# A hybrid decoder block: eight more expert tiles beside the retrieval, two tile buffers instead of four beside the spreading, 80 of the gathered rows moved forward

## The chip, the cores and the metric

One core of one Trainium2 chip runs the whole block in one launch. The metric is device time in microseconds (us); of the kernel before, 3 runs gave a median of 3127.78 us (3124.86 to 3131.33). The core has five engines with a queue each: TensorE (PE, with weight loads shown as PEld), VectorE (DVE), ScalarE (ACT), GpSimd (POOL) and SyncE (SP), which here only issues transfers. Engines wait for one another through semaphores. A queue is worked off in order: while an instruction waits, all behind it wait too.

## The reference

A block of 1024 tokens of width 1024 passes gated linear attention, differential softmax attention and one output projection, and then a retrieval of experts (PEER). The change lies wholly in the last part:

```python
q = (xt @ w_q).reshape(T, 8, 2, 128)                 # 8 heads, 2 sets of sub-keys
s = jnp.einsum('thpd,hpkd->thpk', q, sub_keys)       # 128 scores for each
s_top, i_top = lax.top_k(s, 16)
cand_s = s_top[:, :, 0, :, None] + s_top[:, :, 1, None, :]
best_s, best_pos = lax.top_k(cand_s.reshape(T, 8, 256), 16)
g = jax.nn.softmax(best_s, axis=-1)                  # idx: 16 experts of 16384 for each head
h = jnp.einsum('td,ted->te', xc, jnp.take(u, ic, axis=0))
a = jax.nn.gelu(h, approximate=False) * gc
out = jnp.einsum('te,ted->td', a, jnp.take(v, ic, axis=0))
```

## The kernel before, in words

Of the 8 tiles of 128 tokens, the last 6 (768 tokens) are computed densely: for all 16384 experts, in 128 expert tiles of 128, `gelu(u x)` is multiplied by a dense table of weights that is zero where an expert was not picked, and then by `v`. The first 2 token tiles gather their rows: 256 rows of `peer_u` (128 picks for each of 2 tiles) and 256 of `peer_v`, 512 KB in each gather of 128 experts. Matmuls run on pairs of fp16 parts (three matmuls for one product, lines 238 to 240).

A *u part* of an expert tile is: load `u_in` (512 KB); turn it by 8 transposes (`turn`); ACT splits off `u_hi` and copies `u_all`; POOL forms `u_lo` (`low`); 2 halves of 24 matmuls (`hidden`); gelu. A *v part* is 36 matmuls into `y` for each expert tile. The u part needs no picks, so it can run early, its gelu kept in HBM (`early_tiles`) and read back later. Three stages matter:

- `retrieve` (about 620 to 994 us): for each of 8 heads PE computes queries and scores, and DVE picks (top 16 of the scores twice, candidates, top 16 of them, then index arithmetic); POOL multiplies `match`, DVE sums it. Beside it run 16 early tiles, two per head (`EARLY_R` * 8), one in the first, three in the last. Steps 1 to 3 of pairs of heads are loops.
- `spread_weights` (about 994 to 1526 us): 12 blocks of 64 tokens, each in 16 steps of 4 tokens. In a step DVE builds `same`, `right`, `left`, PE multiplies them into `tab`, ACT copies `tab` to `stage`, and SP stores 2 MB after 8 steps. Beside each block run 4 early tiles (48 in all): the halves of tile b come at steps 4b and 4b+2 of the block, and at step 4b, ahead of the first half, PE turns tile b+1. `EarlyTiles` has 4 buffers here, so that the tile which is turned was loaded a block ahead. SP does, in this order, `keep` (store a gelu, which waits for it) and `load` of the tile four further on. At the end two u tiles (`F.u_in`) for the next stage are turned and the first is multiplied.
- `experts` (about 1526 us to the end): 64 *late* tiles with u and v part, then 64 early ones with the v part alone, and 512 row jobs on DVE (6 per late tile, 2 per early tile), for which POOL issues gathers into 5 row buffers.

`E.turn` waits for `u_loaded`; `E.load` waits for the turn that frees its buffer; `E.keep` waits for `gelu_done`. The lines that the prediction follows:

```python
def turn(self, pe, c, b):
    pe.wait_ge(self.u_loaded[b], c * 16 + 16)
    pe.wait_ge(self.u_all_done, BASE + c * self.ring + b)
def keep(self, queue, c, b):
    queue.wait_ge(self.gelu_done, BASE + 2 * (c * self.ring + b) + 2)
```

Of the kernel before, what the change touches and what calls it, by code (L numbers as in the profile page):

```python
# [1338 lines left out]
EARLY_S = 4  # L1339
BLOCK = 64  # L1340
# [3 lines left out]
N_EARLY = EARLY_R * PEER_H + EARLY_S * NBLOCK  # L1344
# [108 lines left out]
def retrieve(nc, io, T):  # L1453
# [3 lines left out]
    with ExitStack() as ctx:  # L1457
        S = Space(nc, ctx, "r")
        E = EarlyTiles(nc, io, T, S, EARLY_R, 0, EARLY_R * PEER_H)
# [52 lines left out]
        PAIRS = PEER_H // 2  # L1512

        @block.sync
        def _(sp):
            w_v = io.w_peer_q[0].rearrange("(k p) (h c) -> h p k c", p=P, c=QDIM)

            def load_w(h):
                sp.dma_start(w_in[:], w_v[h]).then_inc(w_loaded, 16)

            def step(hh, b, first=False, last=False):
                h = 2 * hh + b
                if not last:
                    sp.wait_ge(w_lo_done, h + 2)
                    load_w(h + 2)
                if not (first and b == 0):
                    E.load(sp, h, 1)
                if not (last and b):
                    E.load(sp, h + 1, 0)
# [6 lines left out]
            for b in range(2):  # L1536
                step(0, b, first=True)
            with sp.Fori(1, PAIRS - 1) as hh:
                for b in range(2):
                    step(hh, b)  # L1540
            for b in range(2):
                step(PAIRS - 1, b, last=True)
            E.all_kept(sp, EARLY_R * PEER_H)

        @block.tensor
        def _(pe):
# [17 lines left out]
            def scores(h, sets=(0, 1)):  # L1564
                for m in sets:
                    pe.wait_ge(q_out, 4 * h + 2 * m + 2)
                    for g in range(2):
                        for j in range(4):
                            t = 4 * g + j
                            last = pe.matmul(bank[2 * m + g][:, j, :], q_t[:, m, t * P:(t + 1) * P],  # L1570
                                             keys_t[:, bass.ds(2 * h + m, 1), :].rearrange("p a k -> p (a k)"),
                                             start=True, stop=True)
                        last.then_inc(scored, 1)

            def step(hh, b, first=False, last=False):
                h = 2 * hh + b
                before = not (first and b == 0)
                if before:
                    E.turn(pe, h - 1, 1)
                else:  # L1580
                    E.turn(pe, h, 0)
                if not (last and b):
                    queries(h + 1, 1 - b)
                    scores(h + 1)
                if before:
                    E.hidden(pe, h - 1, 1, 0)
                    E.turn(pe, h, 0)
                    E.hidden(pe, h - 1, 1, 1)
                E.hidden(pe, h, 0, 0)
                if last and b:  # L1590
                    E.turn(pe, h, 1)
                E.hidden(pe, h, 0, 1)
                if last and b:
                    E.hidden(pe, h, 1, 0)
                    E.hidden(pe, h, 1, 1)
# [8 lines left out]
            for b in range(2):  # L1604
                step(0, b, first=True)
            with pe.Fori(1, PAIRS - 1) as hh:
                for b in range(2):
                    step(hh, b)
            for b in range(2):
                step(PAIRS - 1, b, last=True)  # L1610
            pe.wait_ge(index_done, BASE + 2 * PEER_H)
# [11 lines left out]
        def _(act):  # L1623
# [25 lines left out]
            def step(hh, b, first=False, last=False):  # L1649
                h = 2 * hh + b  # L1650
                before = not (first and b == 0)
                if before:
                    E.split(act, h - 1, 1)
                else:
                    E.split(act, h, 0)
                if not last:
                    split_w(h + 2, b)
                if not (last and b):
                    act.wait_ge(scored, 4 * h + 4)
                    queries_out(h + 1)  # L1660
                    scores_out(h + 1)
                if before:
                    E.gelu(act, h - 1, 1, 0)
                    E.split(act, h, 0)
                    E.gelu(act, h - 1, 1, 1)
                    E.keep(act, h - 1, 1)
                if last and b:
                    E.gelu(act, h, 0, 0)
                    E.split(act, h, 1)
                    E.gelu(act, h, 0, 1)  # L1670
                    E.keep(act, h, 0)
                    for half in range(2):
                        E.gelu(act, h, 1, half)
                    E.keep(act, h, 1)
                act.wait_ge(shifted, h + 1)
                nc.scalar.activation(weight[:], weight[:], ACT.Exp).then_inc(weighted, 1)
                if not (last and b):
                    for half in range(2):
                        E.gelu(act, h, 0, half)
                    E.keep(act, h, 0)  # L1680

# [9 lines left out]
            for b in range(2):  # L1691
                step(0, b, first=True)
            with act.Fori(1, PAIRS - 1) as hh:
                for b in range(2):
                    step(hh, b)
            for b in range(2):
                step(PAIRS - 1, b, last=True)
# [7 lines left out]
        def _(pool):  # L1705
# [6 lines left out]
            def step(hh, b, first=False, last=False):  # L1712
# [781 lines left out]
```

## Time and profile before

| | |
|---|---|
| median of 3 runs | 3127.78 us |
| profiled execution | 3127.37 us, its span 3125.7 us, so 1.67 us around it |
| PE busy | 2975.7 us (95%) |
| DVE busy | 2313.1 us (74%) |
| POOL, ACT busy | 1271.3 us (41%), 993.3 us (32%) |
| granted clock, mean | 0.976 |

Busy shares are means over stages with different limits, so the stretches in the section of rows below are to be read first, and then, within each stage, which engine never waits. The profile names tiles by stage: `r_` is the retrieval, `e_` the spreading, `f_` the experts, `x_` and `p_` are tiles that outlive a stage. In a row of a timeline stand the start, the length, the engine and line, and in brackets how long the engine had been idle before and what released it.

### The profile page before, as it was taken

Reading aid. Unit: us, or ns where it says so; the run is one execution under the profiler, and the core shown is the slowest. Engines: PE = TensorE matmul, PEld = TensorE weight load, DVE = VectorE, ACT = ScalarE, POOL = GpSimd, SP = SyncE. Lnnn points to the kernel's source line nnn. Section 1 sums busy time; section 2 is a strip of 40 time slices with the busy share of each in tenths; the row PEclk is TensorE's granted clock in tenths of the full one; section 3 lists DMA queues with packets and bytes.
Section 4 is the critical chain, followed back from the end, with each engine's and each line's share of the span. In section 5 each row is a group of like instructions: output and inputs, shape, how many; then the busy total and the mean of one; then the engine's idle time right before and its main releaser. Section 6 shows DMA issues by size and latency. Waiting matters only on the chain.

```text
span 3125.7 us, 48327 instructions
## 1 busy us (share of the span) xinstructions
PE 2975.7 (95%) x17450; PEld 1671.2 (53%) x17450; DVE 2313.1 (74%) x4671; ACT 993.3 (32%) x1420; POOL 1271.3 (41%) x875
## 2 busy tenths in 40 slices
PE   7989998899995999999679999999999999999999
PEld 4445464455553777777445555555555554444444
DVE  3355475369997666666388888888888888999996
ACT  4322364234432555555222222222222222222221
POOL 1013011034333121222266666666655655555562
PEclk9999899999997999999889999999999999999999
DMA  3110101212211455555598888888888878888884
GB/s 99 55 54 14 55 1 34 68 60 75 75 36 68 163 201 190 178 186 195 202 319 275 282 272 273 291 285 274 274 273 284 292 258 285 299 305 297 307 290 170
DMA packets 256176, 594.95 MB, mean 190 GB/s; under 512 B 20768, under 2 KB 127408, under 8 KB 252976
## 3 DMA queue, kind: packets, MB, share of 16 engines
q1 hardware_dynamic: 180016, 318.63, 30.3%
q0 software_dynamic: 73728, 268.47, 24.3%
q10 hardware_dynamic: 2304, 6.29, 0.6%
q8 instruction: 62, 1.02, 0.1%
q14 instruction: 66, 0.54, 0.1%
HBM read 513.63 MB, written 79.69 MB: 190 GB/s over the span
## 4 chain that ended last, share of the span: by engine, by line
PE 43%; DMA 3%; DVE 2%; issue 1%; SPq 1%; ACT 0%; POOL 0%; DVEq 0%; ACTq 0%
PE f_y L238 9%; PE f_y L240 9%; PE f_y L239 9%; PE f_hid L238 5%; PE f_hid L239 5%; PE f_hid L240 5%; DMA f_v_in<-in_peer_v 2%; PE f_u_ps L2181 2%; SPq L2147 1%; DMA f_g_in<-dense_weights 1%; DMA f_rows<-in_peer_u,p_row_index 1%; DVE f_rows L2320 1%; DVE p_h L2330 1%; DVE p_h L2312 0%; DVE f_a_lo L2362 0%
## 5 line engine op out<-in xcount | busy, mean ns | idle before, releaser
L238 PE MATMUL f_y<-f_v_hi,f_a_hi 128*128 128x512 f16 x1536 | 583.1, 380 | 12.8 <-DVE p_h L2312 12.7
L239 PE MATMUL f_y<-f_v_lo,f_a_hi 128*128 128x512 f16 x1536 | 582.9, 379 | 0.0
L240 PE MATMUL f_y<-f_v_hi,f_a_lo 128*128 128x512 f16 x1536 | 582.7, 379 | 0.0
L2279 POOL DMA_INDIRECT f_rows<-in_peer_u,p_row_index x256 | 354.2, 1383 | 210.2 <-DVE f_rows L2320 128.5
L2279 POOL DMA_INDIRECT f_rows<-in_peer_v,p_row_index x256 | 310.6, 1213 | 286.0 <-DVE p_h L2330 256.8
L2320 DVE SCALAR_TENSOR_TENSOR f_rows<-f_rows,p_xs 128x1024 f32<-128x1024 f32 x256 | 380.2, 1519 | 50.2 <-DMA f_rows<-in_peer_u,p_row_index 50.2
L2330 DVE SCALAR_TENSOR_TENSOR p_h<-f_rows,f_row_a,p_h 128x1024 f32<-128x1024 f32 x256 | 397.9, 1554 | 20.8 <-DMA f_rows<-in_peer_v,p_row_index 13.9
L2312 DVE SCALAR_TENSOR_TENSOR p_h<-f_y,p_h 128x512 f32<-128x512 f32 x384 | 263.2, 685 | 105.6 <-PE f_y L240 103.3
L2290 POOL TENSOR_TENSOR f_v_lo<-f_v_in,f_v_hi 128x1024 f16<-128x1024 f32 x128 | 281.3, 2197 | 143.9 <-ACT f_v_hi L2254 142.6
L238 PE MATMUL f_hid<-p_act_hi,x_u_hi 128*128 128x384 f16 x1008 | 330.4, 328 | 2.0 <-DVEq L2297 2.0
L239 PE MATMUL f_hid<-p_act_lo,x_u_hi 128*128 128x384 f16 x1008 | 330.4, 328 | 0.0
L240 PE MATMUL f_hid<-p_act_hi,x_u_lo 128*128 128x384 f16 x1008 | 330.0, 327 | 0.0
L1929 DVE TENSOR_TENSOR e_right<-p_iota,p_picked_all 128x512 f16<-128x512 f32 x192 | 138.6, 722 | 181.4 <-PE e_tab L1951 181.4
L1417 POOL TENSOR_TENSOR e_u_lo<-e_u_all,e_u_hi 128x1024 f16<-128x1024 f32 x48 | 106.7, 2223 | 403.7 <-ACT e_u_all L1411 403.7
L238 PEld LDWEIGHTS f_y<-f_v_hi,f_a_hi 128*128 128x128 f16 x1536 | 150.4, 98 | 198.0 <-DVE p_h L2312 21.8
L238 PE MATMUL e_hid<-p_act_hi,e_u_hi 128*128 128x384 f16 x768 | 251.3, 327 | 4.5 <-POOL e_u_lo L1417 4.5
L239 PE MATMUL e_hid<-p_act_lo,e_u_hi 128*128 128x384 f16 x768 | 251.4, 327 | 0.0
L240 PE MATMUL e_hid<-p_act_hi,e_u_lo 128*128 128x384 f16 x768 | 251.3, 327 | 0.0
L240 PEld LDWEIGHTS f_y<-f_v_hi,f_a_lo 128*128 128x128 f16 x1536 | 150.5, 98 | 181.6 <-issue 0.8
L239 PEld LDWEIGHTS f_y<-f_v_lo,f_a_hi 128*128 128x128 f16 x1536 | 150.5, 98 | 176.1 <-issue 0.7
L2261 ACT ACTIVATE f_a_hi<-x_gel 128x768 f16<-128x768 f32 x128 | 107.7, 841 | 332.6 <-DVE x_gel L2354 258.9
L2254 ACT ACTIVATE f_v_hi<-f_v_in 128x1024 f16<-128x1024 f32 x128 | 134.8, 1053 | 196.7 <-DMA f_v_in<-in_peer_v 191.6
(314 smaller groups left out, 5343.0 us busy)
## 6 DMA issues: line engine op xcount, KB each, us to landing
f_v_in<-in_peer_v SPq DMA_DIRECT2D x128, 512.0 KB
dense_weights<-e_stage SPq DMA_DIRECT2D x24, 2048.0 KB, 8.6
f_g_in<-dense_weights SPq DMA_DIRECT2D x32, 1536.0 KB
x_u_in<-in_peer_u SPq DMA_DIRECT2D x64, 512.0 KB
e_u_in<-in_peer_u SPq DMA_DIRECT2D x48, 512.0 KB
x_gel<-early_tiles SPq DMA_DIRECT2D x64, 384.0 KB
early_tiles<-e_gel SPq DMA_DIRECT2D x48, 384.0 KB, 2.5
a_w_in<-in_w_in SPq DMA_DIRECT2D x24, 512.0 KB, 3.7
```

The costliest lines, as they stand in the source:

```text
L238: pe.matmul(out, a_hi, b_hi, start=first, stop=False)
L239: pe.matmul(out, a_hi, b_lo, start=False, stop=False)
L240: return pe.matmul(out, a_lo, b_hi, start=False, stop=last)
L1417: self.nc.gpsimd.tensor_tensor(self.u_lo[b][:], self.u_all[:], self.u_hi[b][:], ALU.subtract).then_inc(self.u_lo_done, 1)
L1929: nc.vector.tensor_tensor(right[r][:], lanes(T.iota[:], 1, P, BANK_T, P), lanes(key1_t[:, toks], 2, P, BANK_T, P), ALU.is_equal)
L2254: nc.scalar.activation(v_hi[g][j][:], v_in[m % 2][:], ACT.Copy).then_inc(v_hi_done, 1)
L2261: nc.scalar.activation(a_hi[g][j][:], gel[m % 2][:], ACT.Copy).then_inc(a_hi_done, 1)
L2279: nc.gpsimd.indirect_dma_start(out=rows[q % ROWS][:], out_offset=None, in_=table, in_offset=bass.IndirectOffsetOnAxis(ap=T.row_index[:, ti ...
L2290: nc.gpsimd.tensor_tensor(v_lo[g][j][:], v_in[m % 2][:], v_hi[g][j][:], ALU.subtract).then_inc(v_lo_done, 1)
L2312: nc.vector.scalar_tensor_tensor(T.h[:, NS + t, cols], y[k % 2][:], 1.0 / S_A, T.h[:, NS + t, cols], ALU.mult, ALU.add).then_inc(y_added, 1)
L2320: nc.vector.scalar_tensor_tensor(row, row, 1.0, T.xs[:, tile, :], ALU.mult, ALU.mult, accum_out=row_hid[:, tile, pick:pick + 1]).then_inc( ...
L2330: nc.vector.scalar_tensor_tensor(T.h[:, tile, :], row, row_a[:, tile, pick:pick + 1], T.h[:, tile, :], ALU.mult, ALU.add).then_inc(row_use ...
```

## The change

- `retrieve` has 24 early tiles in place of 16, given to the heads as 2, 3, 2, 3, 3, 2, 3, 6 (`HEAD_TILES`), and is written out by heads instead of looped. POOL's picks of head h now come in step h+1, behind the first tile's `low`, and the totals of the weights after the next head's first top 16.
- `spread_weights` has 2 buffers of early tiles in place of 4 (`EARLY_RING`), still 4 tiles per block; `right` is built from fp16 copies; DVE does 80 row jobs of the first token tile between its steps, POOL issues their gathers behind each `low`; two more u tiles are loaded for the next stage.
- `experts` has 56 late tiles and 72 early ones; its row jobs are 432, of which 288 lie in the late tiles (5.14 per tile instead of 6) and 2 in each early one. It starts with five rows and tiles 2 and 3 of u loaded, and its first load is `g_in`.

```diff
@@ -1337,11 +1337,17 @@
 EARLY_R = 2
 EARLY_S = 4
+EARLY_RING = 2
+ROWS = 5
+SPREAD_JOBS = 80
...
-N_EARLY = EARLY_R * PEER_H + EARLY_S * NBLOCK
+
+HEAD_TILES = (2, 3, 2, 3, 3, 2, 3, 6)
+N_RETRIEVE = sum(HEAD_TILES)
+N_EARLY = N_RETRIEVE + EARLY_S * NBLOCK
...
+            for h in range(PEER_H):
+                of_head = tiles(h)
+                E.turn(pe, *of_head[0])
+                if h + 1 < PEER_H:
+                    queries(h + 1, (h + 1) % 2)
+                    scores(h + 1)
+                for i, (c, b) in enumerate(of_head):
+                    E.hidden(pe, c, b, 0)
+                    if i + 1 < len(of_head):
+                        E.turn(pe, *of_head[i + 1])
+                    E.hidden(pe, c, b, 1)
...
+            for h in range(PEER_H):
+                of_head = tiles(h)
+                E.low(pool, *of_head[0])
+                if h + 2 < PEER_H:
+                    low_w(h + 2, h % 2)
+                if h:
+                    picks(h - 1)
+                for i, (c, b) in enumerate(of_head[1:]):
+                    E.low(pool, c, b)
+                    if h and i == 0:
+                        weights(h - 1)
+            picks(PEER_H - 1)
+            weights(PEER_H - 1)
...
-        E = EarlyTiles(nc, io, T, S, EARLY_S, EARLY_R * PEER_H, EARLY_S * NBLOCK)
+        E = EarlyTiles(nc, io, T, S, EARLY_RING, N_RETRIEVE, EARLY_S * NBLOCK)
+
+        def ring_at(blk, b):
+
+            return blk * (EARLY_S // EARLY_RING) + b // EARLY_RING, b % EARLY_RING
...
+                for q in range(SPREAD_JOBS * n // ALL, SPREAD_JOBS * (n + 1) // ALL):
+                    row_job(q)
...
                         if half == 0 and b + 1 < EARLY_S:
-                            E.turn(pe, blk, b + 1)
+                            E.turn(pe, *ring_at(blk, b + 1))
                         elif half == 0 and not last:
-                            E.turn(pe, blk + 1, 0)
-                        E.hidden(pe, blk, b, half)
+                            E.turn(pe, *ring_at(blk + 1, 0))
+                        E.hidden(pe, *ring_at(blk, b), half)
...
+            for n in range(BLOCKS_TILES):
+                E.low(pool, *ring_at(n // EARLY_S, n % EARLY_S))
+                upto = SPREAD_JOBS * (n + 1) // BLOCKS_TILES + ROWS if SPREAD_JOBS or n + 1 == BLOCKS_TILES else 0
+                for q in range(fetched, upto):
+                    fetch(q)
...
                 for b in range(EARLY_S):
-                    E.keep(sp, blk, b)
-                    if not last:
-                        E.load(sp, blk + 1, b)
+                    E.keep(sp, *ring_at(blk, b))
+                    if b + EARLY_RING < EARLY_S or not last:
+                        E.load(sp, *ring_at(blk, b + EARLY_RING))
...
-            for b in range(EARLY_S):
+            for b in range(EARLY_RING):
                 E.load(sp, 0, b, again=False)
...
+            for b in range(2):
+                rows = slice((N_EARLY + 2 + b) * P, (N_EARLY + 3 + b) * P)
+                sp.wait_ge(next_turned, b + 1)
+                sp.dma_start(F.u_in[b][:], io.peer_u[0, rows, :]).then_inc(next_loaded, 16)
...
+        LATE_JOBS = JOBS - SPREAD_JOBS - 2 * N_EARLY
...
-            return min(JOBS, 6 * late + 2 * early)
+            return min(JOBS, SPREAD_JOBS + LATE_JOBS * late // EARLY_FROM + 2 * early)
...
-                    if m % GROUP == 0 and not (first and m == 0):
+                    if m % GROUP == 0:
                         load_g(m // GROUP, n)
...
-                    elif not (first and m < 2):
+                    elif not (first and m < 4):
                         sp.wait_ge(u_turned, BASE + n - 1)
...
-            for q in range(ROWS):
-                fetch(q)
```

The change moves instructions on two queues that the prediction speaks of. On SP, at the start of the spreading, `e_u_in` is an early tile's load and `early_tiles<-e_gel` the store of a gelu. Before:

```order
L1387 DMA e_u_in<-in_peer_u 128x1024 x4
L2044 DMA x_u_in<-in_peer_u 128x1024 x2
L2045 UNCONDITIONAL_BRANCH
L2045 ISA
L1391 ISA
L1391 DMA early_tiles<-e_gel 128x768
L1386 REGISTER_ALU
L1387 ISA
L1387 DMA e_u_in<-in_peer_u 128x1024
```

With the change:

```order
L1393 DMA e_u_in<-in_peer_u 128x1024 x2
L2030 DMA x_u_in<-in_peer_u 128x1024 x2
L2031 UNCONDITIONAL_BRANCH
L2031 ISA
L1397 ISA
L1397 DMA early_tiles<-e_gel 128x768
L1392 REGISTER_ALU
L1393 ISA
L1393 DMA e_u_in<-in_peer_u 128x1024
```

The order of stores and loads is the same, but two tiles are loaded ahead of the first store and not four, so the load behind the store of tile n is that of tile n+2 and not n+4.

On POOL, in the last heads of the retrieval, `r_u_lo` is an early tile's `low`, `r_match` the picks and `r_picked` the weights of a head. Before:

```order
L1417 TENSOR_TENSOR r_u_lo<-r_u_all,r_u_hi 128x1024 x2
L1728 TENSOR_TENSOR r_match<-r_match,r_top_f 128x2048 x2
L1731 TENSOR_TENSOR r_picked<-r_weight,r_total 128x8x16
L1417 TENSOR_TENSOR r_u_lo<-r_u_all,r_u_hi 128x1024 x3
L1728 TENSOR_TENSOR r_match<-r_match,r_top_f 128x2048 x2
```

With the change:

```order
L1678 TENSOR_TENSOR r_match<-r_match,r_top_f 128x2048 x2
L1423 TENSOR_TENSOR r_u_lo<-r_u_all,r_u_hi 128x1024
L1683 TENSOR_TENSOR r_picked<-r_weight,r_total 128x8x16
L1423 TENSOR_TENSOR r_u_lo<-r_u_all,r_u_hi 128x1024 x4
L1678 TENSOR_TENSOR r_match<-r_match,r_top_f 128x2048 x2
```

The last head's picks now stand behind the `low` of all six of its early tiles, and the weights of the head before behind that of the second.

## Rows read from the trace of the kernel before

**Rows 1.** Windows: length; busy of PE, PEld, DVE, ACT, POOL; clock; DMA share, GB/s.
```profile
620.00:994.00 374.00, 344.26 (x1954) 200.32 (x1954) 332.23 (x1852) 137.45 (x175) 133.42 (x47) 0.96 0.18 60
994.00:1526.00 532.00, 518.85 (x4288) 364.09 (x4288) 329.09 (x775) 270.80 (x410) 106.69 (x48) 0.98 0.49 180
1526.00:1610.00 84.00, 47.10 (x248) 28.14 (x248) 54.07 (x70) 15.38 (x18) 51.50 (x37) 0.80 0.89 304
1610.00:2596.00 986.00, 985.77 (x5489) 544.48 (x5490) 827.24 (x953) 217.39 (x242) 610.61 (x421) 1.00 0.83 279
2596.00:3122.00 526.00, 519.17 (x2393) 232.60 (x2391) 472.35 (x451) 116.07 (x124) 283.95 (x183) 1.00 0.80 280
```

**Rows 2.** Timeline of one tile's end in the spreading, all engines.
```profile
1145.00 1.06 PE L1951 MATMUL e_tab<-e_right,e_left 128*128 128x128 f16 x16
1145.20 0.49 ACT L1436 ACTIVATE e_gel<-e_hid 128x384 f32<-128x384 f32 x1 [2.90 <-PE e_hid L240]
...
1145.88 0.33 SPq L1391 DMA_DIRECT2D early_tiles<-e_gel  x1
1145.90 1.04 PE L1401 MATMUL e_u_ps<-p_ident,e_u_in 128*128 128x128 f32 x8
...
1146.49 0.35 SPq L1387 DMA_DIRECT2D e_u_in<-in_peer_u  x1
```

**Rows 3.** Timeline of SP, the next tile.
```profile
1156.34 0.33 SPq L1391 DMA_DIRECT2D early_tiles<-e_gel  x1
1156.92 0.35 SPq L1387 DMA_DIRECT2D e_u_in<-in_peer_u  x1
1157.55 0.33 SPq L2037 DMA_DIRECT2D dense_weights<-e_stage  x1
```

**Rows 4.** Windows of 1 us behind the load of rows 2.
```profile
1149.00:1150.00 1.00, 1.00 (x8) 0.59 (x6) 0.06 (x1) 0.01 (x1) 0.91 (x1) 1.00 0.44 176
1150.00:1151.00 1.00, 1.00 (x12) 0.73 (x10) 0.00 (x0) 0.12 (x1) 1.00 (x1) 1.00 0.00 0
```

**Rows 5.** Timeline, a u load early in the experts stage.
```profile
1527.25 0.42 SPq L2150 DMA_DIRECT2D x_u_in<-in_peer_u  x1
...
1535.25 1.96 PE L2181 MATMUL f_u_ps<-p_ident,x_u_in 128*128 128x128 f32 x8 [4.31 <-DMA x_u_in<-in_peer_u]
```

**Rows 6.** Timeline, another idle time of PE.
```profile
1514.32 1.54 PE L1969 MATMUL e_u_ps<-p_ident,x_u_in 128*128 128x128 f32 x8 [2.37 <-DVE x_u_lo L1936]
```

**Rows 7.** Windows just behind the two idle times; PEclk is third from last.
```profile
1514.40:1518.00 3.60, 3.60 (x16) 2.32 (x17) 1.05 (x1) 1.02 (x1) 0.00 (x0) 0.56 0.86 364
...
1535.30:1538.70 3.40, 3.40 (x14) 2.47 (x15) 1.24 (x3) 0.00 (x0) 0.23 (x2) 0.50 1.04 400
```

**Rows 8.** Costliest groups of the page: gathers on POOL, row jobs on DVE.
```profile
L2279 POOL DMA_INDIRECT f_rows<-in_peer_u,p_row_index x256 | 354.2, 1383 | 210.2 <-DVE f_rows L2320 128.5
...
L2320 DVE SCALAR_TENSOR_TENSOR f_rows<-f_rows,p_xs 128x1024 f32<-128x1024 f32 x256 | 380.2, 1519 | 50.2 <-DMA f_rows<-in_peer_u,p_row_index 50.2
```

**Rows 9.** Chain of waits, late tiles: first and last of 58 turns.
```profile
1614.74 0.87 PE f_u_ps L2181 x8
...
2552.01 0.87 PE f_u_ps L2181 x8
```

**Rows 10.** Windows, one head of the retrieval.
```profile
821.90:864.30 42.40, 41.87 (x242) 24.20 (x241) 41.91 (x238) 17.09 (x21) 17.96 (x7) 1.00 0.20 69
```

**Rows 11.** Timeline of PE, the last head's scores.
```profile
917.12 3.73 PE L1570 MATMUL r_bank<-r_keys_t,r_q_t 128*128 128x128 f32 x32
```

**Rows 12.** Timeline of POOL at the end of the retrieval.
```profile
953.60 2.12 POOL L1417 TENSOR_TENSOR r_u_lo<-r_u_all,r_u_hi 128x1024 f16<-128x1024 f32 x1 [8.70 <-ACT r_u_all L1411]
962.84 2.12 POOL L1417 TENSOR_TENSOR r_u_lo<-r_u_all,r_u_hi 128x1024 f16<-128x1024 f32 x1 [7.12 <-ACT r_u_all L1411]
977.29 8.53 POOL L1728 TENSOR_TENSOR r_match<-r_match,r_top_f 128x2048 f16<-128x2048 f16 x2 [12.33 <-DVE r_match L1842]
```

**Rows 13.** Timeline of DVE, the last sum of the retrieval.
```profile
985.86 3.57 DVE L1788 TENSOR_REDUCE r_picked<-r_match 128x128 f32<-128x2048 f16 x1 [0.18 <-POOL r_match L1728]
```

More of the change, by code:

```diff
@@ L1511, in retrieve, with tiles @@
         block = ctx.enter_context(nc.Block())
-        PAIRS = PEER_H // 2
+        def tiles(h):
+            n = sum(HEAD_TILES[:h])
+            return [divmod(i, EARLY_R) for i in range(n, n + HEAD_TILES[h])]
         @block.sync
@@ L1535, in _ @@
             load_w(1)
[L1536 to L1543, printed above, removed]
+            for h in range(PEER_H):
+                if h + 2 < PEER_H:
+                    sp.wait_ge(w_lo_done, h + 2)
+                    load_w(h + 2)
+                for c, b in tiles(h):
+                    if c + 1 < N_RETRIEVE // EARLY_R:
+                        E.load(sp, c + 1, b)
+            E.all_kept(sp, N_RETRIEVE)
         @block.tensor
@@ L1570, in scores @@
                             last = pe.matmul(bank[2 * m + g][:, j, :], q_t[:, m, t * P:(t + 1) * P],
-                                             keys_t[:, bass.ds(2 * h + m, 1), :].rearrange("p a k -> p (a k)"),
-                                             start=True, stop=True)
+                                             keys_t[:, 2 * h + m, :], start=True, stop=True)
                         last.then_inc(scored, 1)
[L1575 to L1595, printed above, removed]
             for r in range(4):
@@ L1603, in _ @@
                 scores(0, sets=(m,))
[L1604 to L1611, printed above, removed]
+            for h in range(PEER_H):
[9 more added lines that the diff above has]
+                    E.hidden(pe, c, b, 1)
+            pe.wait_ge(index_done, 2 * PEER_H)
             pe.wait_ge(weight_done, PEER_H)
@@ L1647, in scores_out, with weigh @@
                                              ACT.Copy).then_inc(s_out, 1)
[L1649 to L1674, printed above, removed]
+            def weigh(h):
                 act.wait_ge(shifted, h + 1)
                 nc.scalar.activation(weight[:], weight[:], ACT.Exp).then_inc(weighted, 1)
[L1677 to L1680, printed above, removed]
             nc.scalar.activation(w_hi[0][:], w_in[:], ACT.Copy, scale=S_W).then_inc(w_hi_done, 1)
@@ L1690, in _ @@
                 scores_out(0, first=True, sets=(m,))
[L1691 to L1697, printed above, removed]
+            for h in range(PEER_H):
+                of_head = tiles(h)
+                E.split(act, *of_head[0])
+                if h + 2 < PEER_H:
+                    split_w(h + 2, h % 2)
+                if h + 1 < PEER_H:
+                    act.wait_ge(scored, 4 * h + 4)
+                    queries_out(h + 1)
+                    scores_out(h + 1)
+                for i, (c, b) in enumerate(of_head):
+                    E.gelu(act, c, b, 0)
+                    if i + 1 < len(of_head):
+                        E.split(act, *of_head[i + 1])
+                    E.gelu(act, c, b, 1)
+                    E.keep(act, c, b)
+                    if i == (len(of_head) - 2 if h + 1 == PEER_H else 1):
+                        weigh(h)
             for r in range(6):
@@ L1813, in step @@
                            for t in range(g * NT // 2, (g + 1) * NT // 2)] for g in range(2)])
-                if not (first and b == 0):
+                if h:
                     dve.wait_ge(weight_done, h)
@@ L1825, in step @@
                 c.step(nc.vector.tensor_scalar(row[0][:], part[:, 0, :], -1.0, 0.0, ALU.add, ALU.max))
-                if not (first and b == 0):
+                if h:
                     for n in range(2):
@@ L2058 @@
 NE = NKEYS
-ROWS = 5
 def experts(nc, io, T):
@@ L2367, in step @@
                 row_jobs(2)
+            lo_u(2, 2)
+            lo_u(3, 3)
             for n in range(NE):
@@ L2434, in allocate_first @@
     F.gel = [S.sb(f"gel{b}", [P, DSEQ], side="right") for b in range(2)]
+    F.rows = [S.sb(f"rows{b}", [P, D], side="right") for b in range(ROWS)]
     return F
```

206 lines of the change are left out of this document (106 added, 100 removed).

## The prediction

> **What bounds the kernel now.** I read the windows by stage first [rows 1]. In the retrieval PE is busy 344 of 374 us and DVE 332, so both are near their limit; in the spreading PE is busy 519 of 532 us and DVE only 329; in the experts stage PE is busy without a break in the late tiles (986 of 986) and nearly so in the early ones (519 of 526), while its first 84 us hold 47 us of work. So PE sets the end everywhere. A u part moved to another stage is worth something only where PE stood idle there, and any new idle time of PE costs its full length.
>
> Then I read one tile of the spreading on all engines [rows 2], because the change halves the buffers there. At 1145.00 PE ends the second half of tile n and multiplies two steps of tables; ACT does the gelu at 1145.20; SP stores it at 1145.88 and issues the next load at 1146.49; PE had begun the turn of tile n+2 at 1145.90. One tile later the store comes at 1156.34 [rows 3], a period of 10.46 us.
>
> **Spreading: the load now comes behind the turn that needs it.** Before, the load at 1146.49 was for tile n+4, with two more tile periods to land. With two buffers it is for tile n+2, and the code still turns tile n+2 at step 4(n+1), two steps behind the last half of tile n. That is the turn at 1145.90, 0.59 us ahead of the issue. SP cannot be earlier, since the load stands behind the `keep` of tile n, which waits for its gelu, which waits for PE. PE waits in order, and behind the turn stand the two halves of tile n+1 and its tables, so everything stops. It happens for tiles 2 to 47: 46 times.
>
> The wait per tile is 0.59 us plus issue to landing. Lower end: the store of 384 KB and the load of 512 KB move together until about 1149.4 (in 1149 to 1150 the transfers are at a share of 0.44, in the next us at 0.00) [rows 4], 2.9 us from issue, so 3.5 us. Upper end: a u load issued at 1527.25 behind two `v` loads, with gathers beside it, was waited for until 1535.25, 8.0 us [rows 5], so 8.6 us. In the changed spreading there are 1.67 gathers of 512 KB per tile beside the load, and every second load has the 2 MB store issued 0.63 us behind it [rows 3], but the mean share of the transfers was 0.49 [rows 1], not near 1 as in the rows of the upper end. I take 4.5 us, near the quiet end.
>
> The idle time costs clock as well. After PE had been idle 2.37 and 4.31 us [rows 5, 6], the granted clock was 0.56 and 0.50 in the next 3.6 and 3.4 us of full work [rows 7], that is the lower of its two levels (1.2 instead of 2.4 GHz) for nearly all of them: half of about 3.4 us, 1.7 us of work lost each time. I take 1.7 us per wait; the ends are 0 (the clock might stay up where waits come regularly) and 3.4 us (two such stretches).
>
> The Trainium skill, "TensorE: Matmul & The Clock Gate", section "HAM oscillation — how this bites in real kernels", describes a kernel in which a DMA wait per K-tile made every K-tile start at the lower clock, and prices it as the throttled time times one half. By that rule each of the 46 waits would pay; the two gaps of this trace agree, but no stretch here has gaps that repeat.
>
> The same notes, "DMA: Bandwidth & Descriptors", section "Anatomy of one DMA — SWDGE (gpsimd) path", give 2.0 us plus bytes / 436e3 (in us) for a transfer. For 512 KB that would be an estimate of 3.2 us, or 3.8 us of wait; this trace has 2.9 to 8.0 us, and the sum goes by these.
>
> Sum: 46 x (4.5 + 1.7) = 285 us. DVE does not replace PE as the bound: its 329 us plus 80 row jobs of 1.52 us [rows 8], 122 us, are 451 us in a stage of some 815 us. The two added u loads are issued with a u part of PE still ahead, 8.7 us (below), more than the 8.0 us of the upper end; cost 0, bound 5. The POOL gathers lie in idle time (107 of 532 us busy).
>
> **Experts: eight u parts fewer.** A late tile takes 16.44 us (58 turns from 1614.74 to 2552.01) [rows 9]. The early stretch of 526 us [rows 1] holds 64 tiles and the last group of 4, 68 v parts, 7.74 us each. So a u part is 8.70 us, and eight of them take 69.6 us off this stage: the 72 early tiles keep 2 row jobs each, as before, and the late ones have fewer, so PE stays the bound in both. The start is worth more than it looks: 84 us hold 47 us of PE work [rows 1], with the transfers at 0.89. Now five rows and two u tiles (3.5 MB) are there, `g_in` is loaded first, and 5.14 gathers per tile run instead of 6. At the stretch's 304 GB/s the 3.5 MB are 11.5 us, and 0.86 gathers of 0.52 MB less in five tiles another 7. I take 20 us; ends 0 and 37 (all idle time).
>
> **Retrieval: 8 u parts more.** In the middle heads PE is busy 41.87 of 42.4 us, with DVE at 41.91 [rows 10]. There a third tile lengthens the head by its full price, since PE had no room. Before the last head's scores (917.12) [rows 11] lay 11 tiles, now 15: at 8.7 to 9.24 us, 36 us later, 957 us for their end at 920.8. Behind them come 3 + 6 = 9 tiles. Tiles in a row take 9.24 us (`low` at 953.60 and 962.84) [rows 12], because `low` waits for the split and the next half for `low`: 83 us, so PE ends at 1040 us. DVE's index sums ended at 989.4 [rows 13], 68.6 us behind the scores; with the same distance they would end at 1026 (a few us later if DVE waits for the weights that now stand behind the `low` of the second tile), but its picks on POOL now stand behind the `low` of the sixth tile, at about 1032: 8.5 us of picks [rows 12] and one sum of 3.6 us [rows 13] make 1044.5. Against 989.4 that is 55 us. Ends: 40 (69.6 us of work less the 30 us for which PE was idle in the whole stage [rows 1]) and 62.
>
> So the move itself pays 70 + 20 - 55 = 35 us, and the halved buffers take 285.
>
> **Sum.** Against the profiled execution, 3127.4 us (its span and 1.7 us around it, 0.4 us under the median): 3127.4 + 285 - 69.6 - 20 + 55 = 3377.8 us, 8.0% slower.
>
> **Rivals.**
> 1. *Waits without the clock's share.* The clock stays high where matmuls return every 15 us. For it: in the middle of the retrieval, with short gaps, the clock is 1.00 [rows 10]. Against it: two of two gaps over 2 us [rows 7]. 46 x 4.5 = 207: 3300 us.
> 2. *Loads as slow as at the experts' start.* Gathers and the 2 MB store fill the transfers just when the u load is waited for: 46 x (8.6 + 1.7) = 474: 3567 us. Against it: the mean share of 0.49, and a longer period lowers it.
> 3. *POOL as a second wait.* Each `low` now stands behind gathers that wait for DVE's row jobs. If DVE lies less than a tile ahead, `low` comes late. `low` takes 2.12 us [rows 12] and the gathers 1.67 x 1.38 us [rows 8], 4.4 us per tile: at worst 46 x 4.4 = 202 more, 3580 us. Against it: during PE's wait DVE catches up, and POOL has over 10 us per tile.
> 4. *The other side: faster.* The wait for the load is hidden after all, because the load is issued or lands earlier than the turn. Then 3127.4 - 35 = 3093 us, 1.1% faster. It decides at 35 / 46 = 0.76 us of wait and clock per tile; over that the change loses. Against it stands that the issue alone is 0.59 us behind the turn [rows 2], and 3.5 us is the least a landing allows.
>
> **Chances.** Forecast (about 3378, from 3320 to 3450) 0.62; rival 1 0.18; rivals 2 and 3 together 0.16, much of it part of the way (3450 to 3530); rival 4 0.03; 0.01 for about no change. The range 3260 to 3500 takes in rival 1 with a gap of 3.7 us and leaves out the far parts of 2 and 3. Anything beyond 0.2% either way can be told from no change here: faster 0.03, same 0.01, slower 0.96.
>
> **What would show it.** In the waits of the changed profile, PE (or its weight loads) on line 1407, `e_u_ps`, waits for the load `e_u_in` 46 times, 4 to 5 us each; the period of the stores `early_tiles<-e_gel` is near 16.7 us, not 10.46; the clock of the spreading falls from 0.98 to near 0.85; the stage lasts some 815 us. The retrieval ends near 1050 us, with PE busy nearly to the end, and the last `r_match` behind the last `r_u_lo`. The experts stage has 52 steady periods of 16.44 us and starts its `f_y` within 65 us. If the store's period is still 10.5 us, the forecast is wrong at its root; if waits are there but the clock stays 1.00, it is rival 1.

## The result: 10.7% slower, and where the time went

The changed kernel takes 3465.47 us (median of 4 runs, 3451.03 to 3471.21) against 3126.86 us for the kernel before on the same chip: a ratio of 1.107, with a 95% interval of 1.104 to 1.111. The forecast was 3378 us with a range of 3260 to 3500. The profiled execution took 3451.03 us, so it is the shortest of the four; its span is 3449.3 us, 323.6 us over the span before (3125.7). The medians differ by 338.6 us: what the trace adds up to below is some 15 us less than the median.

First the page of the changed kernel: busy times, the granted clock by slices, the group of the turn and the landing of its load (last column of the last row, us from issue).

```profile
PE 3067.0 (89%) x17450; PEld 1719.2 (50%) x17450; DVE 2316.9 (67%) x4665; ACT 977.3 (28%) x1417; POOL 1266.7 (37%) x883
...
PE   7999889899996676667666699999999999999999
...
PEclk9999899999997888888888799999999999999999
...
L1407 PE MATMUL e_u_ps<-p_ident,e_u_in 128*128 128x128 f32 x384 | 91.9, 419 | 259.3 <-DMA e_u_in<-in_peer_u 258.2
...
e_u_in<-in_peer_u SPq DMA_DIRECT2D x48, 512.0 KB, 4.9
```

Eleven slices in the middle show a PE at six and seven tenths and a clock of 0.7 to 0.8: that is the spreading. The windows by stage (retrieval from 620, spreading, first part of the experts, late tiles, early tiles) answer to [rows 1]:

```profile
core 0: us, PE busy (x) PEld busy (x) DVE busy (x) ACT busy (x) POOL busy (x), PEclk, DMA share, GB/s
620.00:1050.00 430.00, 409.19 (x2385) 239.40 (x2382) 345.54 (x1851) 158.97 (x205) 145.63 (x55) 1.00 0.20 67
1050.00:1936.00 886.00, 621.36 (x4291) 420.56 (x4292) 421.70 (x937) 243.07 (x388) 183.85 (x133) 0.84 0.46 159
1936.00:2000.00 64.00, 37.32 (x222) 23.45 (x220) 42.18 (x57) 14.33 (x16) 39.18 (x25) 0.76 0.85 281
2000.00:2855.00 855.00, 855.00 (x4767) 472.40 (x4765) 670.33 (x739) 188.81 (x210) 488.07 (x324) 1.00 0.75 253
2855.00:3447.00 592.00, 584.65 (x2694) 261.79 (x2692) 536.67 (x510) 131.89 (x141) 324.84 (x208) 1.00 0.81 282
```

The spreading grew from 532 to 886 us. PE's busy time in it went from 519 to 621 us for nearly the same number of matmuls: each takes longer because the clock is 0.84, not 0.98. Its idle time went from 13 to 265 us. The waits of PE in that stretch name the cause (us in all, times, longest):

```profile
PE e_u_ps L1407 <- DMA e_u_in<-in_peer_u: 258.2, 47, 6.8
PE e_u_ps L1939 <- DVE x_u_lo L1906: 2.4, 1, 2.4
...
PE e_hid L238 <- POOL e_u_lo L1423: 1.1, 1, 1.1
```

The kernel before has this wait once, for the very first tile (4.8 us). One tile on SP, and the turn of PE that waits for its load, answer to [rows 2, 3]:

```profile
1365.03 0.33 SPq L1397 DMA_DIRECT2D early_tiles<-e_gel  x1
1365.64 0.35 SPq L1393 DMA_DIRECT2D e_u_in<-in_peer_u  x1
1382.12 0.33 SPq L1397 DMA_DIRECT2D early_tiles<-e_gel  x1
1382.70 0.35 SPq L1393 DMA_DIRECT2D e_u_in<-in_peer_u  x1
1383.34 0.33 SPq L2023 DMA_DIRECT2D dense_weights<-e_stage  x1
```

```profile
1381.26 1.06 PE L1921 MATMUL e_tab<-e_right,e_left 128*128 128x128 f16 x16
1389.06 1.97 PE L1407 MATMUL e_u_ps<-p_ident,e_u_in 128*128 128x128 f32 x8 [6.75 <-DMA e_u_in<-in_peer_u]
```

PE has nothing to do from 1382.3. The load is issued at 1382.70, with the 2 MB store 0.64 us behind it, and the turn starts at 1389.06, 6.36 us after the issue. The clock around this wait, before it, behind it and after:

```profile
1381.00:1389.00 8.00, 1.31 (x19) 1.04 (x17) 5.01 (x13) 1.53 (x3) 0.96 (x1) 0.87 0.76 236
1389.00:1393.40 4.40, 4.34 (x17) 2.93 (x18) 0.00 (x0) 1.94 (x2) 0.16 (x1) 0.50 0.88 376
1393.40:1398.00 4.60, 4.60 (x39) 3.10 (x38) 1.22 (x3) 1.53 (x3) 2.93 (x2) 0.97 0.17 24
```

For 4.4 us after the wait PE works at its lower level (0.50, that is 1.2 GHz), which costs 2.2 us. The turn itself takes 1.97 us there. It is so at every tile: in the trace's record of the granted clock the lower level follows each of the 47 waits, and PE works 2.7 to 6.1 us at it before the clock is back.

By the starts and ends of the same instructions in both traces, the 323.6 us are made of: up to the end of the retrieval +57.3 (`p_row_index` at 1046.80, was 989.5); spreading +351.5; from the last `e_tab` to the first `f_hid` -0.1; experts -85.0. The retrieval itself grew by more than 57.3: its first `r_bank` matmul starts at 619.4 here and at 624.8 before, so the stage is 62.7 us longer. The code ahead of it is the same in both, and in the traces of this study it ends anywhere from 616.8 to 625.3; a difference of a few us between the ends of one stage in two traces says little.

### The profile page after: what moved, and what is told of

The parts are those of the page before. It is cut to its first block and busy times, and to the rows that moved or that the text cites. A ratio compares the mean times of both kernels' runs of the same rounds, so it can differ in the third digit from the quotient of the medians.

```text
span 3449.3 us, 46781 instructions
## 1 busy us (share of the span) xinstructions
PE 3067.0 (89%) x17450; PEld 1719.2 (50%) x17450; DVE 2316.9 (67%) x4665; ACT 977.3 (28%) x1417; POOL 1266.7 (37%) x883
## 5 line engine op out<-in xcount | busy, mean ns | idle before, releaser
L1897 DVE TENSOR_TENSOR e_right<-e_iota,e_key 128x512 f16<-128x512 f16 x192 | 134.7, 702 | 435.3 <-PE e_tab L1921 435.3
L2287 POOL DMA_INDIRECT x_rows<-in_peer_v,p_row_index x256 | 316.1, 1235 | 273.2 <-DVE p_h L2337 245.7
L2337 DVE SCALAR_TENSOR_TENSOR p_h<-x_rows,f_row_a,p_h 128x1024 f32<-128x1024 f32 x256 | 394.0, 1539 | 9.8 <-DMA x_rows<-in_peer_v,p_row_index 2.8
L1407 PE MATMUL e_u_ps<-p_ident,e_u_in 128*128 128x128 f32 x384 | 91.9, 419 | 259.3 <-DMA e_u_in<-in_peer_u 258.2
L238 PE MATMUL f_hid<-p_act_hi,x_u_hi 128*128 128x384 f16 x880 | 287.8, 327 | 2.1 <-DVEq L2303 2.1
L240 PE MATMUL f_hid<-p_act_hi,x_u_lo 128*128 128x384 f16 x880 | 287.8, 327 | 0.0
L239 PE MATMUL f_hid<-p_act_lo,x_u_hi 128*128 128x384 f16 x880 | 287.7, 327 | 0.0
L2287 POOL DMA_INDIRECT x_rows<-in_peer_u,p_row_index x171 | 252.3, 1475 | 92.7 <-DVE x_rows L2327 53.1
L2327 DVE SCALAR_TENSOR_TENSOR x_rows<-x_rows,p_xs 128x1024 f32<-128x1024 f32 x176 | 268.0, 1560 | 9.0 <-DMA x_rows<-in_peer_u,p_row_index 8.9
L1407 PEld LDWEIGHTS e_u_ps<-p_ident,e_u_in 128*128 128x128 f32 x384 | 73.2, 218 | 266.8 <-issue 242.9
```

Of the source, the lines that this page charges most:

```text
L238: pe.matmul(out, a_hi, b_hi, start=first, stop=False)
L239: pe.matmul(out, a_hi, b_lo, start=False, stop=False)
L240: return pe.matmul(out, a_lo, b_hi, start=False, stop=last)
L1407: last = pe.transpose(self.u_ps[:, k, :], self.u_in[b][:, k * P:(k + 1) * P], self.T.ident[:])
L1897: nc.vector.tensor_tensor(right[r][:], lanes(iota1[:], 1, P, BANK_T, P), lanes(key1[:, toks], 2, P, BANK_T, P), ALU.is_equal)
L2287: nc.gpsimd.indirect_dma_start(out=rows[q % ROWS][:], out_offset=None, in_=table, in_offset=bass.IndirectOffsetOnAxis(ap=T.row_index[:, ti ...
```

## Experiments

All times are medians; each ratio is to the kernel before on the same chip, with its 95% interval.

**1. The load ahead of the store.** The changed kernel, with one edit in SP's step of the spreading: the load of tile n+2 no longer stands behind the store of tile n.

```diff
                 for b in range(EARLY_S):
-                    E.keep(sp, *ring_at(blk, b))
                     if b + EARLY_RING < EARLY_S or not last:
                         E.load(sp, *ring_at(blk, b + EARLY_RING))
+                    E.keep(sp, *ring_at(blk, b))
```

> The changed kernel with one pair of lines swapped: in the spreading SP issues the load of tile n+2 ahead of the store of tile n, not behind it. It then waits only for the turn of tile n, a whole tile period before the turn that needs it. My theory: the 5.5 us wait and the 2.2 us of clock per tile both vanish, 46 x 7.7 = 354 us, and what is left is the move itself: about 3465 - 354 = 3110 us, from 3085 to 3125, with a store period of 10.46 us and the clock of the spreading at 0.98 or more. Rival, that the transfers (gathers, stores) or POOL's and DVE's added work slow the spreading: the wait moves elsewhere, the period stays over 13 us and the time over 3220 us.

Measured: 3121.33 us (12 runs), ratio 0.998 (0.997 to 1.000). The window over its spreading, and PE's two longest waits there:

```profile
1050.00:1582.00 532.00, 516.64 (x4228) 359.51 (x4229) 517.57 (x935) 242.83 (x384) 184.39 (x133) 0.98 0.73 259
```

```profile
PE e_u_ps L1407 <- DMA e_u_in<-in_peer_u: 9.2, 9, 5.2
PE e_tab L1921 <- DVE e_left L1901: 4.9, 9, 0.9
```

The same buffers, the same work, and 344 us less than the changed kernel. On SP a load still stands behind a store, as before; only which tile the load is for differs:

```profile
1300.44 0.33 SPq L1397 DMA_DIRECT2D early_tiles<-e_gel  x1
1301.04 0.33 SPq L2023 DMA_DIRECT2D dense_weights<-e_stage  x1
1301.66 0.35 SPq L1393 DMA_DIRECT2D e_u_in<-in_peer_u  x1
1310.92 0.33 SPq L1397 DMA_DIRECT2D early_tiles<-e_gel  x1
1311.51 0.35 SPq L1393 DMA_DIRECT2D e_u_in<-in_peer_u  x1
```

The load at 1301.66 is for the turn at 1311.55, one tile period later. Its buffer was freed by the turn that starts at 1290.01, a period earlier still, so the load could go sooner: what holds it back now is the store of tile n-1 ahead of it in the queue, and the swap of two lines gave it one period more and not two. The margin is small: 9.9 us from issue to turn for a landing of 8.4 us in the median (3.4 to 11.6). This load came just too late (PE waited 0.24 us for it). Of the 9.2 us of wait 5.2 are the first tile's, which the kernel before has too; the other eight waits add up to 4.0.

**2. Two buffers in the kernel before**, with the 16 tiles in the heads and no gathers in the spreading.

```diff
-        E = EarlyTiles(nc, io, T, S, EARLY_S, ...)
+        E = EarlyTiles(nc, io, T, S, EARLY_RING, ...)
...
-                    E.keep(sp, blk, b)
-                    if not last:
-                        E.load(sp, blk + 1, b)
+                    E.keep(sp, *ring_at(blk, b))
+                    if b + EARLY_RING < EARLY_S or not last:
+                        E.load(sp, *ring_at(blk, b + EARLY_RING))
```

> The kernel before with two buffers of early tiles in the spreading in place of four, and nothing else of the change. My theory: the same wait as in the changed kernel, without gathers somewhat shorter (landing 4.0 us, wait 4.6, clock 2.0): 46 x 6.6 = 304, so 3127 + 304 = 3431 us, from 3390 to 3480. Rival, that the wait needs the gathers of rows beside it: a wait of 3.5 us and little clock, under 3310 us.

Measured: 3426.78 us (4 runs), ratio 1.096 (1.094 to 1.099). Its wait for the load and its spreading:

```profile
PE e_u_ps L1402 <- DMA e_u_in<-in_peer_u: 211.5, 47, 5.1
```

```profile
994.00:1811.00 817.00, 601.99 (x4221) 400.05 (x4222) 319.26 (x772) 268.46 (x405) 106.21 (x48) 0.85 0.31 114
```

This edit alone carries the loss: 299 us, 6.5 us per tile. Every second load has the 2 MB store behind it, and those take longer: from the issue of the load to the turn pass 3.7 us in the median without that store and 4.4 us with it (23 loads each; in the changed kernel 4.7 and 5.8 us).

**3. Two buffers in the kernel before, with the load ahead of the store**: the edits of 1 and 2 together.

> The kernel before with two buffers of early tiles in the spreading, and the load of tile n+2 issued ahead of the store of tile n. My theory is that not the number of buffers costs, but that the load stands behind the gelu in SP's queue: the time is that of the kernel before, 3127 us within 0.3%. Rival, two buffers are too few in themselves: the period stays above 11 us and the time over 3150 us.

Measured: 3127.36 us (10 runs), ratio 0.999 (0.998 to 1.001). PE's wait for `e_u_in` after the first tile is a single one of 0.3 us, and the window 994 to 1526 reads almost as before:

```profile
994.00:1526.00 532.00, 519.03 (x4288) 363.78 (x4288) 328.94 (x775) 270.81 (x410) 106.53 (x48) 0.98 0.49 180
```

So two buffers are enough. What cost the time is that the order on SP's queue was left as it was for four.

**4. Matmuls in the wait.** The changed kernel, with 20 matmuls of no use to the result, 512 columns each, ahead of the wait for the load in the turn (the turn's other wait, for `u_ps`, which they overwrite, goes ahead of them):

```diff
+        pe.wait_ge(self.u_all_done, BASE + c * self.ring + b)
+        for _ in range(self.fill):
+            pe.matmul(self.u_ps[:, 0:4, :]..., self.T.act_hi[:, 0, 0:P], self.T.act_hi[:, 0, 0:HALF], ...)
         pe.wait_ge(self.u_loaded[b], c * 16 + 16)
-        pe.wait_ge(self.u_all_done, BASE + c * self.ring + b)
```

> The changed kernel, but PE does 20 matmuls of 512 columns (4.3 us, their result is overwritten by the transposes) before each wait for the load in the spreading. The load lands when it did, so the wait and the fill overlap. If the excess of 102 us in PE's busy time is clock, the clock goes back to nearly 1.00 and the period from 18.1 to about 16 us: 46 x 2.1 = 97 us less, about 3368 us, 3350 to 3400. If it is not clock but something that comes with the wait, the time stays at 3465 us.

Measured: 3378.94 us (4 runs), ratio 1.080 (1.077 to 1.083), 86.5 us less than the changed kernel. One tile on PE and its spreading:

```profile
1314.27 4.48 PE L1407 MATMUL e_u_ps<-p_act_hi 128*128 128x512 f16 x20
1320.36 1.09 PE L1411 MATMUL e_u_ps<-p_ident,e_u_in 128*128 128x128 f32 x8 [1.61 <-DMA e_u_in<-in_peer_u]
```

```profile
1060.00:1853.00 793.00, 730.07 (x5168) 451.11 (x5167) 412.41 (x925) 238.92 (x383) 187.33 (x133) 0.98 0.49 172
```

The loads still come as late, but the clock is back at 0.98 and the turn takes 1.09 us instead of 1.97. Without the added matmuls (212 us in this window) PE's busy time is 518 us, against 621 in the changed kernel and 519 before: the whole excess of 102.5 us was clock. Of it 86.5 us come back in the time, 1.9 us per tile. That missed the middle of the expectation by 11 us, since the loads here land a little later than I had taken (5.3 us in the median).

**5. No gathers in the spreading.** The changed kernel with `SPREAD_JOBS = 0`, so that all row jobs lie in the experts stage.

> The changed kernel with no row jobs in the spreading (SPREAD_JOBS = 0): all 512 lie in the experts stage, 6.57 per late tile. It tells what the gathers beside the load cost. My theory: landing goes from 4.9 us to about 4.0 and the wait from 5.5 to 4.6: 46 x 0.9 = 41 us less; the late tiles stay bound by PE at 16.44 us, the start costs some 5 us more: about 3430 us, 3405 to 3450. Rival, that the wait is set by the 2 MB store and the latency alone: 3465 us or a few more. Rival, that the 80 jobs back in the late tiles lengthen them (DVE at 90%): over 3480 us.

Measured: 3424.53 us (4 runs), ratio 1.095 (1.092 to 1.097). PE's wait and the page's row of the load's landing:

```profile
PE e_u_ps L1407 <- DMA e_u_in<-in_peer_u: 219.5, 47, 6.0
```

```profile
e_u_in<-in_peer_u SPq DMA_DIRECT2D x48, 512.0 KB, 4.1
```

It is 41 us less than the changed kernel, for 0.8 us less of landing at each tile. The edit takes DVE's 80 row jobs out of the spreading together with their gathers; that it is the gathers which count here is read from the landing, not shown by itself. In the trace the spreading is 48.0 us shorter, and the experts stage, which has the jobs back, 17.4 us longer. With the load first the same question has another answer:

**6. The load first, and no gathers** (experiment 1 with `SPREAD_JOBS = 0`).

> The changed kernel with the load ahead of the store, and no row jobs in the spreading: all 512 in the experts stage. Against the same kernel with 80 in the spreading (3121 us) it tells what moving them is worth. My theory: nothing that can be measured, since PE sets the late tiles either way and the start waits for u tile 4: 3116 to 3126 us. Rival, that the gathers moved forward relieve the start: over 3128 us.

Measured: 3119.64 us (11 runs), ratio 0.998 (0.997 to 0.999), against 0.998 for experiment 1. Moving 80 row jobs into the spreading is worth nothing that can be told in the time, but the traces show that it has a price and a gain that about cancel. From the end of the retrieval to the last `e_tab` the spreading takes 520.4 us without the jobs, as long as in the kernel before (521.3), and 535.0 us with them in experiment 1, where DVE is busy 518 us of it; the experts stage takes 1528.4 us with all the jobs and 1520.8 us in experiment 1.

**7. The load first, and 16 tiles in the heads** (experiment 1 with `HEAD_TILES = (2,) * 8`).

> The changed kernel with the load ahead of the store, and 16 early tiles in the retrieval (two for each head) in place of 24. Against the same kernel with 24 (3121 us) it tells what the eight moved u parts are worth. My theory: the retrieval gets about 54 us shorter and the experts stage 70 us longer: 3121 + 16 = 3137 us, from 3128 to 3145. Rival, that the retrieval has room for the eight tiles and the gain is lost elsewhere: over 3160 us. Rival, that they are worth nothing: 3121 us.

Measured: 3138.88 us (11 runs), ratio 1.004 (1.002 to 1.005). Against experiment 1 it is 17.6 us slower. Eight u parts in the retrieval instead of the experts are therefore worth 17.6 us. By the traces the retrieval ends at 1011.0 with 16 tiles and at 1046.5 with 24; counted each from its own first `r_bank`, it takes 385.7 and 429.7 us, so the eight tiles cost it 44.0 us.

The same trace shows something else. The retrieval before has 16 tiles too, and takes 364.7 us. Written out by heads, with its tiles two to a head, it takes 21 us more for the same work: PE is idle for 29.5 us at its end, waiting for DVE's last sums, where the kernel before has 16.5 us. So not all of the retrieval's growth is the eight tiles. What part of the rewriting costs it, the order of the instructions or the tiles' places, no run here separates.

**8. The two u tiles ahead of the `v` tiles at the experts' start.** In the profile after, the 64 us of the start have 26.7 us in which PE waits for `x_u_in`. On SP:

```profile
1935.01 0.38 SPq L2130 DMA_DIRECT2D f_g_in<-dense_weights  x1
1935.44 27.13 SPq L2143 DMA_DIRECT2D f_v_in<-in_peer_v  x4
1962.61 0.56 SPq L2130 DMA_DIRECT2D f_g_in<-dense_weights  x1
1963.22 4.67 SPq L2141 DMA_DIRECT2D x_u_in<-in_peer_u  x1
```

Four `v` tiles, of which the last two wait for a free buffer, and the second `g_in` stand ahead of u tile 4. The edit, on top of experiment 1:

```diff
+                    elif first and m in (2, 3):
+                        sp.wait_ge(u_turned, BASE + m + 1)
+                        sp.dma_start(u_in[m % 2][:], u_v[view, m + 2]).then_inc(u_loaded[m % 2], 16)
-                    elif not (first and m < 4):
+                    elif not (first and m < 6):
```

> The changed kernel with the load ahead of the store, and at the start of the experts stage the loads of u tiles 4 and 5 issued ahead of those of v tiles 2 and 3, not behind v tile 3 and the second g_in. There PE waited 34.7 us for u tile 4. My theory: the term of the start that was missing (20 us forecast, 7 and 0 measured) comes back: first f_y 15 to 25 us earlier, about 3101 us, from 3093 to 3110. Rival, that the start is bound by the volume of transfers and the wait goes to v or g_in: 3115 to 3125 us.

Measured: 3110.71 us (5 runs), ratio 0.994 (0.993 to 0.996). From the first `f_hid` to the first `f_y` it takes 57.2 us, against 71.7 in experiment 1; the whole is 10.6 us less. What remains there is 20.9 us of another wait, one queue further on:

```profile
PE f_u_ps L2173 <- DVE x_u_lo L2313: 20.9, 1, 20.9
```

I had expected 3093 to 3110, so it missed by 0.7 us.

**9. The last picks one tile earlier.** The retrieval's end in the profile after, on POOL and on DVE, answers to [rows 12, 13]:

```profile
1033.44 2.12 POOL L1423 TENSOR_TENSOR r_u_lo<-r_u_all,r_u_hi 128x1024 f16<-128x1024 f32 x1 [7.12 <-ACT r_u_all L1417]
1035.53 7.63 POOL L1678 TENSOR_TENSOR r_match<-r_match,r_top_f 128x2048 f16<-128x2048 f16 x2
```

```profile
1039.39 7.38 DVE L1745 TENSOR_REDUCE r_picked<-r_match 128x128 f32<-128x2048 f16 x2 [1.08 <-POOL r_match L1678]
1046.80 0.43 DVE L1815 SCALAR_TENSOR_TENSOR p_row_index<-r_picked 128x256 uint32<-128x256 f32 x1
```

The edit puts `picks` of the last head ahead of the sixth tile's `low` on POOL, and the sums ahead of `totals` on DVE, on top of experiment 8:

```diff
                 for i, (c, b) in enumerate(of_head[1:]):
+                    if h + 1 == PEER_H and i == len(of_head) - 2:
+                        picks(h)
                     E.low(pool, c, b)
...
-            picks(PEER_H - 1)
...
-            totals(PEER_H - 1)
             for n in range(2):
                 index_sum(PEER_H - 1, n)
+            totals(PEER_H - 1)
```

> As the one before, and in the last head POOL does the picks ahead of the sixth tile's low instead of behind it, and DVE the index sums ahead of the totals. My theory: the tail behind PE's last half in the retrieval is 8 us of picks and sums; they now end 5 to 6 us earlier, and low moves by under 1 us: about 5 us (0.16%) less than the one before. Rival, that the totals, which wait for the gelu of the fifth tile, set the end: no difference.

Measured: 3109.55 us (5 runs), ratio 0.993 (0.992 to 0.995), 1.2 us less than experiment 8 with intervals that overlap: inconclusive. In the trace `p_row_index` comes at 1043.67 instead of 1052.49, but between experiments 1 and 8, which are alike up to there, it shifted by 6 us as well (1046.5 to 1052.5). Behind the picks PE still has the sixth tile to finish, so an earlier index alone need not help it; that is argued, not shown. This is nevertheless the fastest version of the study, 0.66% under the kernel before.

## Why the prediction was right, and what was mis-sized

The measured 3465.5 us lie inside the stated range, but not in the 3320 to 3450 that I called the forecast: they lie in the stretch from 3450 to 3530 that I had given to rivals 2 and 3, part of the way. The mechanism is the forecast's, with some of rival 2 in it. Of the 88 us between 3377.8 and the median, 66 are the two terms of the halved buffers, some 7 the experts and the retrieval, and 14 lie between the profiled execution and the median of its kernel, which the trace can't explain.

**The mechanism held.** The load stands behind the store of tile n, comes behind the turn that needs it, and PE waits in order: 47 waits in the profile, one of them the first tile's that was there before; 46 were forecast. Experiment 2 shows that this part alone loses 299 us, and experiments 1 and 3 that it vanishes with the order on SP.

**The wait: forecast 4.5 us per tile, measured 5.5** (idle time grew by about 251 us over 46 tiles). I chose the value near the quiet end, from transfers that were over 2.9 us behind the issue [rows 4]. The median landing was 4.9 us. Experiment 5 gives the parts: 4.1 us without the gathers, 0.8 more with them. Without gathers, in experiment 2, the wait is 4.5 us on average, just what I had taken for the kernel with them. So the quiet end itself (3.5 us) was too low, and what I had put on top of it was used up before the gathers came. Two things were missing from it. The end of the transfers is not yet the landing: for a load of experiment 2 with the same store of 384 KB ahead of it, issued at 1157.01, the transfers' share falls to 0.16 at 1160.0 and to 0.01 at 1160.2, and the turn that waits for it starts at 1160.75. And the loads with the 2 MB store behind them take another 0.7 us (1.1 in the changed kernel; the medians are with experiment 2). The Trainium skill, "DMA: Bandwidth & Descriptors", section "Anatomy of one DMA — SWDGE (gpsimd) path", gave an estimate of 3.2 us. It states its formula for transfers that GpSimd issues, and SyncE issues this load; 4.1 and 4.9 us were measured, and the measurement decides.

**The clock: forecast 1.7 us per tile, measured 2.2** (PE's busy time in the stage grew by 102.5 us). The mean of 0.84 is what was forecast (0.85), over a longer stage. Each wait is followed by a stretch at the lower level; the one shown is 4.4 us long, against 3.4 and 3.6 in [rows 7], and over all tiles they are 2.7 to 6.1 us. Experiment 4 takes away the idle time and not the late load, and gets 86 us back, so it is the idle time that lowers the clock. Together with the wait that is 7.7 us instead of 6.2 per tile, 66 us more than the sum had. The rule of the Trainium skill, "TensorE: Matmul & The Clock Gate", section "HAM oscillation — how this bites in real kernels", was that each wait pays with a stretch at half speed; the trace agrees, at 47 of 47 waits.

**The retrieval: forecast +55, measured +57.3 at its end and +62.7 in its own length.** That the end came within 2.3 us of the sum is in part luck, since the stage began 5.4 us earlier in this trace; its own length lies at the upper end that I gave (62). The path was as forecast: the last head's scores end at 955.6 (957 in the sum), the last `r_match` starts the moment the last `r_u_lo` ends (1035.53), and two sums and the index follow. PE was busy 409 of 430 us.

**Eight u parts out of the experts: forecast -69.6, and the start -20; measured -85.0 together.** Of it the start gave 6.7 us (71.3 to 64.6 from the first `f_hid` to the first `f_y`), so the tiles gave 78. The start is the second term of the wrong size. I had priced it by what the transfers had less to carry; but PE waits for u tile 4, and its load stands behind two `v` loads that wait for a buffer and behind the second `g_in`. Fewer bytes ahead of it don't help while those waits remain; experiment 8 moved the load and got 14.5 us of the start. So the move pays less than the 35 us of the sum: 27.7 by this trace (85.0 less 57.3), 17.6 for the eight u parts by themselves (experiment 7), and some 6 for the whole change against the kernel before once the load comes first (experiment 1).

**The rivals.** Rival 1 (waits without the clock's share) falls by the clock of 0.84 and by experiment 4. Rival 2 (8.6 us of wait) would need the loads to land in 8.0 us; they took 4.9. It was right in direction: the gathers of the spreading cost 0.8 us per load, and every second load, which has the 2 MB store behind it, takes 0.7 to 1.1 us more. Landings of 8.4 us do occur, in experiment 1, where the transfers are at 0.73 instead of 0.46, but there hardly anything waits for them (4.0 us in all). Rival 3 (POOL) falls by the waits: `e_hid` waited for `e_u_lo` once, 1.1 us. Rival 4 (faster) falls by the rows: PE has nothing to do from 1382.3, and the load is issued at 1382.70. Experiment 1 makes the case that it describes, and came to 0.2% faster, 28 us short of the 3093 us that I gave it. The start accounts for 20 us of this: it takes 71.7 us there, as before. The spreading is also 13.7 us longer than before, and experiment 6, in which it is not, puts that on the 80 row jobs and their gathers.

What stays open is why the stretch at the lower level is longer at some tiles than at others: no run here varied the length of the wait by itself. With waits of 4.5 us (experiment 2) PE's busy time grew by 83 us, 1.8 us per tile, and with 5.5 us by 2.2, but there the gathers differ too. Experiment 4 gives a hint: PE still has 22 idle times of 1.5 to 2.9 us in its spreading, and only 9 of them are followed by the lower level. The 20 us between the changed kernel's runs stay open too, but they are nothing special: 22 runs of the kernel before, on another chip, lie 18.9 us apart.

## What to carry to other kernels

When a ring of buffers gets shorter, read the order on the queue that loads it again: a load that stands behind a store of the newest result is tied to the end of that compute, and with few buffers that is already behind the point where its data is wanted. Put the load behind what frees its buffer (here the turn) and ahead of the store; two buffers were then as good as four here. The order of the remaining stores and loads still sets the margin, as the 9.9 us against 8.4 of experiment 1 show. And a wait of 5 us in every tile costs more than 5 us: count the slower work that follows it too, and where the wait can't go, know that in this kernel the idleness cost the clock (experiment 4).

## What the runs showed of the hardware that I had not expected

- The same 512 KB load took 4.1 us to land without gathers, 4.9 with gathers beside it and 8.4 when the whole stage ran 40% shorter, with the gathers, and the transfers were at 0.73. With the stage as short but without the gathers it was 3.9 (experiment 6, transfers at 0.50). The landing that a profile shows for a hidden load is no price for the same load once it is waited for.
- The loads that have a 2 MB store issued 0.6 us behind them take longer, though they were issued first: 4.4 us instead of 3.7 from issue to turn (experiment 2). No run takes the store away by itself.
- In the load of experiment 2 that was looked at closely, the transfers' share had fallen to 0.01 by 1160.2, and PE, waiting for it, started at 1160.75.
- The lower clock returned after every one of 47 waits, for 850 us; the chip did not settle at a level for a pattern that repeats. Twenty matmuls in each wait kept it at 0.98.
- The comparison that builds `e_right` from f16 copies (line 1897) took 702 ns for 128x512, hardly less than the 722 ns before; the narrower input gained it 3%.
